# Matrix-memory heads of the odd mixer: weights summed over key blocks on VectorE before one ones-matmul, and values multiplied ahead of denominators

## The reference

```
w_intra = jnp.exp(dmat - m_t[..., None])            # decay weights, causal
sw      = w_intra * einsum('...ld,...sd->...ls', q, k)
num     = einsum('...ls,...sv->...lv', sw, v)  + state part
den_raw = jnp.sum(sw, axis=-1)                 + state part
den     = jnp.maximum(jnp.abs(den_raw), jnp.exp(-m_t))
hc      = num / den[..., None]
hm      = rmsnorm_2(sigmoid(o_m) * hc, ml_norm_g)
```

## Time and profile before

| | us |
|---|---|
| median of 3 runs | 2757.64 |
| the profiled execution | 2757.27 |
| its span (first to last instruction in the trace) | 2755.3 |
| TensorE busy | 2718.4 (99%) |
| VectorE busy | 1537.2 (56%) |
| ScalarE busy | 1110.5 (40%) |

### The profile page before, as it was taken

How to read it: one execution, slowest core, us unless ns; L and a number is a source line. 1 busy time by engine, 2 the same in 40 slices (tenths; PEclk the granted TensorE clock), 3 DMA queues, 4 the chain that set the end, 5 groups by cost and what they waited for, 6 DMA issues and landing times.

```text
span 2755.3 us, 33598 instructions
## 1 busy us (share of the span) xinstructions
PE 2718.4 (99%) x12697; PEld 2228.6 (81%) x12697; DVE 1537.2 (56%) x2107; ACT 1110.5 (40%) x1516; POOL 40.8 (1%) x36
## 2 busy tenths in 40 slices
PE   8999999999999999999999999999999999999998
PEld 7887788888888778888888888888878678788887
DVE  5376855456635685554567664434564556644344
ACT  3246544334313654532352443323343654532223
POOL 3000000000200000000000000000000000000000
PEclk9999999999999999999999999999999999999999
DMA  5322233332332123333243423333343123233322
GB/s 163 92 62 61 84 94 94 95 101 84 105 106 71 53 62 107 91 95 103 80 122 92 116 84 92 95 103 91 91 108 85 48 70 123 77 92 91 107 80 88
DMA packets 466510, 252.02 MB, mean 91 GB/s; under 512 B 22670, under 2 KB 460903, under 8 KB 466287
## 3 DMA queue, kind: packets, MB, share of 16 engines
q1 hardware_dynamic: 466415, 250.70, 31.6%
HBM read 248.54 MB, written 2.11 MB: 91 GB/s over the span
## 4 chain that ended last, share of the span: by engine, by line
PE 91%; DVE 5%; ACT 3%; issue 1%; DMA 0%; ACTq 0%; SPq 0%; DVEq 0%
PE M L750 26%; PE M L752 26%; PE M L751 26%; DVE w_lo L2139 1%; PE M L838 1%; PE M L836 1%; PE M L837 1%; PE A L935 1%; PE A L910 1%; PE A L982 1%; PE A L924 0%; PE A L750 0%; PE A L752 0%; PE A L751 0%; DVE prob L2593 0%
## 5 line engine op out<-in xcount | busy, mean ns | idle before, releaser
L750 PE MATMUL M<-h_hi,w_hi 128*128 128x512 f32 x2184 | 859.6, 394 | 0.8 <-issue 0.7
L752 PE MATMUL M<-h_hi,w_lo 128*128 128x512 f32 x2184 | 850.2, 389 | 0.0
L751 PE MATMUL M<-h_lo,w_hi 128*128 128x512 f32 x2184 | 850.1, 389 | 0.0
L1519 ACT ACTIVATE w_hi<-stage 128x1024 fp32r<-128x1024 f32 (+3 forms) x504 | 497.1, 1026 | 714.2 <-PE M L752 589.4
L2139 DVE TENSOR_TENSOR w_lo<-stage,w_hi 128x1024 fp32r<-128x1024 f32 (+3 forms) x504 | 589.6, 1205 | 165.2 <-ACT w_hi L1519 164.5
L750 PEld LDWEIGHTS M<-h_hi,w_hi 128*128 128x128 f32 x2184 | 409.9, 188 | 89.8 <-issue 3.9
L752 PEld LDWEIGHTS M<-h_hi,w_lo 128*128 128x128 f32 x2184 | 409.8, 188 | 86.5
L751 PEld LDWEIGHTS M<-h_lo,w_hi 128*128 128x128 f32 x2184 | 410.0, 188 | 85.8 <-issue 2.6
L750 PE MATMUL M<-hid_hi,w_hi 128*128 128x512 f32 x704 | 274.8, 390 | 0.2 <-DVE w_lo L2139 0.2
L752 PE MATMUL M<-hid_hi,w_lo 128*128 128x512 f32 x704 | 274.0, 389 | 0.0
L751 PE MATMUL M<-hid_lo,w_hi 128*128 128x512 f32 x704 | 273.9, 389 | 0.0
(11 more groups left out here) (488 smaller groups left out, 3214.0 us busy)
## 6 DMA issues: line engine op xcount, KB each, us to landing
stage<-in_w_up SPq DMA_DIRECT2D x88, 512.0 KB, 4.4
stage<-in_ffn_w_gate_up SPq DMA_DIRECT2D x88, 512.0 KB, 4.5
stage<-in_w_in SPq DMA_DIRECT2D x80, 512.0 KB, 4.6
stage<-in_w_down SPq DMA_DIRECT2D x32, 384.0 KB, 3.7
stage<-in_ffn_w_down SPq DMA_DIRECT2D x32, 384.0 KB, 3.6
stage<-in_od_w_in SPq DMA_DIRECT2D x21, 512.0 KB, 3.9
stage<-in_w_down SPq DMA_DIRECT2D x32, 320.0 KB, 3.3
stage<-in_ffn_w_down SPq DMA_DIRECT2D x32, 320.0 KB, 3.3
```

Of the source, the lines that this page charges most:

```text
L750: pe.matmul(bank, a_hi, b_hi, start=(n == 0), stop=False)
L751: pe.matmul(bank, a_hi, b_lo, start=False, stop=False)
L752: last = pe.matmul(bank, a_lo, b_hi, start=False, stop=(n == k - 1))
L1519: act.activation(w_hi[:, s, part * HALF:part * HALF + n], stage[:, part, 0:n], ACT.Copy)\
```

## The change

In `ml_weighted`, VectorE adds four instructions for each head after the three multiplications. The first waits until these have ended (and from head 1 on, until the ones-matmul of the head before has read `g_top`). It copies the first 128 columns of block 0 into `g_top`; the others add block 1 on columns 128 to 511, block 2 on 256 to 511, block 3 on 384 to 511. `g_top` is a 128 x 512 tile that earlier held rows of the gates. `ml_sw_done` now counts two a head.

In `ml_values`, TensorE multiplies the values first (four matmuls into A[0]) and then `ones` with `g_top`, one matmul of 512 columns, into A[1]. It waits for `g_top` in between. In `ml_read`, ScalarE copies the numerators first and takes the absolute value second, and TensorE waits for that second one (`ml_abs`) where it waited for `ml_num_out`. `ml_weights(h)` waits for `ml_d` of head h - 2, which is now the later of the two semaphores.

```diff
             def ml_values(h):
 
-                pe.wait_ge(ml_sw_done, h + 1)
+                pe.wait_ge(ml_sw_done, 2 * h + 1)
                 w = ml_w[:, h % 2, :]
-                for st in range(TT):
-                    last = pe.matmul(A[1][:, st * P:], ones, w[:, ST[st]:ST[st] + ST_N[st]],
-                                     start=(st == 0), stop=(st == TT - 1))
-                last.then_inc(ml_d, 1)
                 for st in range(TT):
                     last = pe.matmul(A[0][:, st * P:], v_ml[:, st, h * P:(h + 1) * P], w[:, ST[st]:ST[st] + ST_N[st]],
                                      start=(st == 0), stop=(st == TT - 1))
                 last.then_inc(ml_nd, 1)
+                pe.wait_ge(ml_sw_done, 2 * h + 2)
+                pe.matmul(A[1][:, :], ones, g_top[:, :], start=True, stop=True).then_inc(ml_d, 1)
...
-            pe.wait_ge(ml_num_out, 1)
+            pe.wait_ge(ml_abs, 1)
             ml_score(1)
...
                 act.wait_ge(ml_diag_done, h + 1)
                 if h >= 2:
-                    act.wait_ge(ml_nd, h - 1)
+                    act.wait_ge(ml_d, h - 1)
...
             def ml_read(h):
 
+                act.wait_ge(ml_nd, h + 1)
+                if h >= 2:
+                    act.wait_ge(ml_out, h - 1)
+                act.activation(ml_num[h % 2][:, :], A[0][:, :], ACT.Copy).then_inc(ml_num_out, 1)
                 act.wait_ge(ml_d, h + 1)
                 if h:
                     act.wait_ge(ml_hm, h)
                 act.activation(ml_1[:, :], A[1][:, :], ACT.Abs).then_inc(ml_abs, 1)
-                act.wait_ge(ml_nd, h + 1)
-                if h >= 2:
-                    act.wait_ge(ml_out, h - 1)
-                act.activation(ml_num[h % 2][:, :], A[0][:, :], ACT.Copy).then_inc(ml_num_out, 1)
...
                 last.then_inc(ml_sw_done, 1)
 
+                if h:
+                    dve.wait_ge(ml_d, h)
+                dve.wait_ge(ml_sw_done, 2 * h + 1)
+                dve.tensor_copy(g_top[:, 0:P], w[:, 0:P])
+                link(dve.tensor_tensor(g_top[:, P:], w[:, P:S], w[:, ST[1]:ST[1] + ST_N[1]], ALU.add))
+                link(dve.tensor_tensor(g_top[:, 2 * P:], g_top[:, 2 * P:], w[:, ST[2]:ST[2] + ST_N[2]], ALU.add))
+                dve.tensor_tensor(g_top[:, 3 * P:], g_top[:, 3 * P:], w[:, ST[3]:ST[3] + ST_N[3]], ALU.add)\
+                   .then_inc(ml_sw_done, 1)
```

More of the change, by code:

```diff
@@ L1362, in _ @@
             latent_tiles(q0 + 1, cq_hi, cq_lo, 3)
-            pe.wait_ge(ml_num_out, 2)
+            pe.wait_ge(ml_abs, 2)
             ml_score(2)
@@ L1372, in _ @@
             ml_square_sum(1)
-            pe.wait_ge(ml_num_out, 3)
+            pe.wait_ge(ml_abs, 3)
             ml_score(3)
@@ L1446, in _ @@
             pe.wait_ge(rounded_set, 2 * DEPTH + 2)
-            pe.wait_ge(ml_num_out, ML_HEADS)
+            pe.wait_ge(ml_abs, ML_HEADS)
             pe.wait_ge(m_free, k0 + 3)
```

## The result

The changed kernel takes 2764.76 us (median of 10 runs, 2763.56 to 2767.79), the kernel before 2757.85 us (median of 10). The ratio is 1.0023, with a 95% interval of 1.0015 to 1.0031: slower, by 6.3 us going by the ratio and 6.9 by the medians, where 2758.6 and a range up to 2762.2 had been forecast. The ratio is estimated from all runs of a comparison and need not be the quotient of two medians; two slow executions of the kernel before in the later comparisons, of 6102.62 and 4721.99 us, are left out of it. The profiled execution of the changed kernel took 2767.79 us, the longest of its runs; its span is 2766.0 us.

A forecast was written before the change was run, and what follows sets the result against it. TensorE was taken to bound the program, but VectorE, then ScalarE, the changed stretch's second half. Profiled 2757.27 + 0.46 (chain) + 0.8 + 0.6 - 0.5 (clock) gave 2758.6 us, range 2755.0 to 2762.2.

The forecast's parts named there:

- TensorE's saving: TensorE, each head: four ones-matmuls replaced by one of 512 columns save 1.30 us, 5.2 us in all as the ceiling.
- A block of additions: VectorE, each head: copy and three additions cost 1.53 us, with bounds of 1.3 and 1.8 us.
- The gaps: TensorE, before the square sums of heads 1 and 2: idle times of 0.64 and 0.66 us become some 3.5 us each.
- The net of +0.46 us: Chain up to the first latent score: 2.6 us saved against 2 x 1.53 us on VectorE, so 0.46 us later.
- the failed step: Clock terms: half clock behind the two new gaps, +0.8 and +0.6 us, and -0.5 us for the fall at 2200.
- +0.8 and +0.6: Half clock behind the two gaps: +0.8 us at head 3's scores (at most 2.2), +0.6 at first latent scores (at most 2.7).
- -0.5 for the fall at 2200: Near 2200: the existing clock fall, costing about 1.3 us, may not happen again so soon, so 0.5 us is gained.
- the second term: First latent scores behind the second gap: half clock adds 0.6 us, between nothing and 2.7 us.
- The clock takes it all: Rival: half clock over all of head 3's scores and the first latent scores, +5.4 us, 2762.6 us; chance 0.13.
- The saving stays: Rival: slack in VectorE's sequence lets TensorE keep more, up to -5.2 us, likeliest 2755.5 us; chance 0.17.
- Additions are dearer: Rival: VectorE's block costs 1.8 us, net +1.0 in place of +0.46 us, 2759.4 us; chance 0.1.
- The chance of 0.06: Whole kernel slower by over 5.5 us (0.2%), taken as the worse half of the clock case.

The follow-up runs named there:

- e1: Changed kernel plus three useless 512-column matmuls ahead of the square sums of heads 1 and 2, filling both gaps: 2759.07 us, ratio 1.0003 to before.
- e2: Kernel before plus only the four VectorE additions a head, their result unread and TensorE's work unchanged: 2765.44 us, ratio 1.0021 to before.
- e6: Changed kernel with three useless matmuls in the second gap alone, ahead of head 2's square sum: 2759.62 us, ratio 1.0004 to before.
- e3: Changed kernel without VectorE's additions; the one ones-matmul reads block 0 of the weights alone: 2759.61 us, ratio 1.0006 to before.
- e10: Changed kernel with heads 2 and 3's additions moved off VectorE's path and head 3's ones-matmul later, no useless matmuls: 2761.11 us, ratio 1.0005 to before.
- e5: Changed kernel with three useless matmuls in the first gap alone, ahead of head 1's square sum: 2762.21 us, ratio 1.0012 to before.
- e7: Changed kernel with both gaps filled, plus useless matmuls before head 3's square sum and the first latent scores: 2756.97 us, ratio 0.9991 to before.
- e8: Kernel before with one useless matmul before head 3's square sum and three before the first latent scores: 2755.75 us, ratio 0.9988 to before.
- e9: Changed kernel with heads 2 and 3's additions moved off VectorE's path, head 3's ones-matmul later, and gaps filled with useless matmuls: 2755.89 us, ratio 0.9985.
- e11: Changed kernel with additions moved and gaps filled, two useless matmuls instead of one before head 2's square sum: 2755.09 us, ratio 0.9988 to before.
- e4: Kernel before with the order alone changed: values first, then four ones-matmuls, numerators read first, no additions: 2759.30 us, ratio 1.0007 to before.

## Why the prediction was wrong

**The work and the chain: right.** TensorE's saving was 1.30 us for each of heads 0 and 1: from the values to head 2's scores it was 20.84 us and is 18.23 (2159.26 - 2141.03), 2.61 less. A block of additions was put at 1.53 us and is 1.58; the copy overlaps, as counted, for the first addition starts 0.14 us after it (2150.11) and it lasts 0.23. The gaps were put at 3.5 us and are 3.52 and 3.51. The net of +0.46 us up to the first latent score is +0.52 in e1, where the clock holds almost that far (to 2194.1), and the two blocks alone are 3.16 us in e2, against 3.06. Two of four savings end as idle time, the other two pay for VectorE: shown.

**The clock: the failed step.** The prediction took both gaps for long enough to bring half clock, and then sized what that costs by "+0.8 and +0.6, less than half, because the clock will partly have recovered by the time the scores run, and -0.5 for the fall at 2200". In the profiled execution head 3's scores took 2.0 us more (4.43 for 2.42), not 0.8. The two sets of latent scores took not 0.6 but 5.0 us more: from 2195.83 to the end of the second set, at 2206.10, it is 10.3 us, where it was 5.2. Of these, 3.4 us are left at the next maxima. Three errors lie in the second term.
- Its upper bound counted head 0's latent scores alone, 2.7 us. Head 1's follow directly, VectorE waits for them too, and the clock stayed low over both.
- The recovery was taken from the one short fall in the trace. There the work behind it is different; here the clock stayed at 0.50 for 13.65 us of nearly unbroken TensorE work.
- Nothing was allowed for what is late next. The weight split stands behind the maxima of head 1 on VectorE, the DMA of the next chunk behind the split, and this transfer of 5.41 us came onto the chain.

The -0.5 had the wrong sign. The idle time of 1.82 us behind which the clock had fallen at 2200 is gone, but the long stretch lies over the same place, and further falls came at 2225 and 2328.

The span of the profiled execution is 10.7 us longer than that of the one before, and adds up to: 1.3 ahead of head 0's values; 0.5 on VectorE's chain and 2.2 at head 3's scores in the middle; 3.4 with the long stretch; 0.7 with the fall at 2225; 2.3 at the late weight chunk; 0.3 behind it. It is the longest of ten, and its first and its last two terms (3.9 us) have not been tied to the change. The failed step, the clock terms, thus measured 2.2 us at head 3 (1.6 in e6) where 0.8 was put, and 3.4 to 4.1 us from the first latent score to 2248 where 0.6 - 0.5 = 0.1 was put.

**The rivals.** "The clock takes it all" was the right mechanism, priced at 2762.6 and given 0.13; that price lay just outside the stated range, and with one set of latent scores in it was still 2 us too low. It should have been the forecast. What it says of itself, that "it needs the worst timing twice", does not hold for the second gap: e1's, e3's and e10's executions have the long stretch after gaps of 0.9 to 2 us. "The saving stays" needed slack on VectorE's chain, and e2 refutes it: both blocks of additions stand in its middle in full, 3.16 us. "Additions are dearer" was wrong, they cost 1.58 us; its 2759.4 us was also added up wrongly, as its terms give 2759.2. The chance of 0.06 for slower by over 0.2% was too small; the measured time is 0.23% over before.

The 6.9 us between the medians thus are: 0.5 on VectorE's chain, and 5.7 that go when both gaps are filled (2764.76 to 2759.07), which e5 and e6 divide without sharp bounds, the larger part to the second gap. The remaining 0.7 us are argued: e1's two runs above 2762 have a mean granted clock of 0.995, the other nine 0.997 or more, and one of the two is the profiled execution with its long stretch, so they are put down to falls that e1 still has in some executions. In e7 no run is above 2758.82. What e7 gains beyond e1, 0.0012 by the ratios, the kernel before was losing too: e8 stands 0.0012 below it.

## What to carry to other kernels

Where TensorE waits for another engine, work taken from TensorE is worth nothing there, and the idle time that it leaves can cost more than the work did: look at what the granted clock does after the gaps that the trace already has, and price a new gap by all the work that follows it, up to the next place where TensorE is not waited for, and by the transfer that starts behind that. A saving can also be waited away again at a later transfer, as in the traces of e9 and e11. A few useless matmuls in a gap into a bank that is overwritten next are a cheap test of it, and in this kernel a gain. Work that is moved to a busy engine has to be put behind what the others wait for; to put it where its input is ready cost twice 1.58 us.

## What the runs showed of the hardware

The clock stayed at 1.2 GHz with TensorE busy 12.59 of 13.65 us in the latent scores (matmuls on 96 rows with short ones of 128 columns between them), and in e1, e2, e3, e5 and e10 for about 13.7 us (17 in e5) over the same code. After the falls at the first gap it was back after 3.4 us (e3, e6) and 6.8 us (changed kernel), during head 3's scores or at their end. Gaps of 0.9 and 1.4 us close together brought a fall in e1's profiled execution and none in e6's, and gaps of 2.22 us (e2) and 2.49 us (e10) brought none. The gap of 1.82 us before the square sum of head 3 brought one in the kernel before and none in e4 and e6. The kernel before differs between its own executions: over 2755.58 to 2763.8 us beside e8, which with its two gaps filled spreads over 2753.59 to 2756.93. What in the work keeps the clock low over the latent scores was not tried.
